# Condition rows loaded first, fourteen of them before the dilated attention, and the attention stores between the two maxima

## What is computed

```python
mod_l = (jax.nn.silu(c) @ w_ada[layer] + b_ada[layer])[:, None, :]
mod_c = jax.nn.silu(c_ctx) @ w_ada[layer] + b_ada[layer]
sh1_l, sc1_l, g1_l, sh2_l, sc2_l, g2_l = jnp.split(mod_l, 6, axis=-1)
...
h_l = modulate(x_l, sh1_l, sc1_l)
```

```python
s_win = jnp.einsum('bhwd,bhrwcd->bhwrc', q_row, k_win).astype(F32) * scale + bias
s_ctx = jnp.einsum('bhwd,bhsd->bhws', q_row, k_ctx).astype(F32) * scale
s = jnp.concatenate([s_win.reshape(b, h, GRID_W, n_win), s_ctx], axis=-1)
p = jax.nn.softmax(s, axis=-1).astype(v.dtype)
...
return (jnp.einsum('bhwrc,bhrwcd->bhwd', p_win, v_win)
        + jnp.einsum('bhws,bhsd->bhwd', p[..., n_win:], v_ctx))
```

## Time and profile before

| | |
|---|---|
| median of 3 runs | 2664.65 us (2660.22 to 2666.28) |
| the profiled execution, its time | 2659.06 us |
| its span, first to last instruction | 2657.3 us |
| busy: PE, DVE, ACT, POOL | 95%, 57%, 35%, 31% of the span |
| mean granted TensorE clock | 0.964 of full speed |
| DVE on condition rows in `dil_project` | 32 instructions, from 49.77 us |
| first scores of the dilated attention | 118.67 us |
| neighbourhood attention | from 1185 to 1291 us |

### The profile page before, as it was taken

The page is one execution under the profiler, slowest core; times in us unless marked ns, Lnnn a source line. Parts: engine busy times, 40 slices in busy tenths (PEclk is TensorE's granted clock), DMA queues, the critical chain, the costliest instruction groups (busy, mean ns, idle before and its releaser), DMA issues.

```text
span 2657.3 us, 37269 instructions
## 1 busy us (share of the span) xinstructions
PE 2515.0 (95%) x14492; PEld 2064.5 (78%) x14492; DVE 1503.9 (57%) x2134; ACT 934.1 (35%) x1414; POOL 834.8 (31%) x445
## 2 busy tenths in 40 slices
PE   6799899999999989998999999999998997999998
PEld 5567887888888877866788888888876755788887
DVE  4756745635755878486455456654675466534242
ACT  3357213322223646335433222122255421433231
POOL 2334002354442222223223333222223321354443
PEclk9899988999997999999999999999998998999999
DMA  5512001434431110231013233422311110232222
GB/s 192 198 41 87 11 1 64 164 134 152 167 134 56 48 48 1 62 74 16 17 48 125 98 111 126 143 88 95 127 64 46 40 72 24 80 111 96 101 96 79
DMA packets 78567, 228.49 MB, mean 86 GB/s; under 512 B 21456, under 2 KB 23504, under 8 KB 77786
## 3 DMA queue, kind: packets, MB, share of 16 engines
q1 hardware_dynamic: 66504, 182.36, 20.0%
q10 hardware_dynamic: 11922, 44.15, 4.9%
HBM read 224.37 MB, written 2.12 MB: 85 GB/s over the span
## 4 chain that ended last, share of the span: by engine, by line
PE 83%; DVE 7%; issue 4%; ACT 3%; POOL 1%; DMA 1%; SPq 0%; DVEq 0%; ACTq 0%; POOLq 0%
PE ps L271 21%; PE ps L272 21%; PE ps L273 21%; PE ps L768 3%; PE ps L783 3%; PE ps L799 2%; PE ps L439 1%; PE ps L391 1%; POOL w_lo L2407 1%; DVE probs L1062 1%; DVE rstd L680 1%; PE ps L2232 1%; DVE small L860 1%; PE ps L448 1%; ACT probs L832 1%
## 5 line engine op out<-in xcount | busy, mean ns | idle before, releaser
L2407 POOL TENSOR_TENSOR w_lo<-ring,w_hi 128x1024 fp32r<-128x1024 f32 x293 | 712.9, 2434 | 1445.6 <-ACT w_hi L264 942.4
L271 PE MATMUL ps<-act_hi,w_hi 128*128 128x512 f32 x2280 | 843.4, 370 | 16.1 <-DVE mix_lo L950 11.0
L273 PE MATMUL ps<-act_hi,w_lo 128*128 128x512 f32 x2280 | 829.9, 364 | 0.0
L272 PE MATMUL ps<-act_lo_ffn,w_hi 128*128 128x512 f32 (+1 forms) x1408 | 512.8, 364 | 0.0
L271 PEld LDWEIGHTS ps<-act_hi,w_hi 128*128 128x128 f32 x2280 | 430.2, 189 | 100.5 <-issue 21.1
L273 PEld LDWEIGHTS ps<-act_hi,w_lo 128*128 128x128 f32 x2280 | 429.0, 188 | 72.2
L264 ACT CAST w_hi<-ring 128x1024 fp32r<-128x1024 f32 (+1 forms) x167 | 174.0, 1042 | 724.9 <-PE ps L273 633.9
L1137 ACT CAST w_hi<-ring 128x1024 fp32r<-128x1024 f32 (+1 forms) x132 | 137.5, 1043 | 459.8 <-PE ps L273 459.8
L272 PEld LDWEIGHTS ps<-act_lo_ffn,w_hi 128*128 128x128 f32 x1408 | 265.1, 188 | 41.9 <-issue 0.7
L271 PE MATMUL ps<-hidden_hi,w_hi 128*128 128x512 f32 x704 | 256.3, 364 | 1.8 <-DVE hidden_lo L1218 1.5
L1062 DVE SCALAR_TENSOR_TENSOR ada_place<-ada_place 128x1024 f32<-128x1024 f32 x160 | 245.6, 1535 | 20.3 <-DMA ada_place<-in_w_ada 6.6
(11 more groups left out here) (369 smaller groups left out, 3387.1 us busy)
## 6 DMA issues: line engine op xcount, KB each, us to landing
ring<-in_w_ffn SPq DMA_DIRECT2D x204, 512.0 KB, 3.2
ada_place<-in_w_ada ACTq DMA_DIRECT2D x80, 512.0 KB, 4.3
ada_place<-in_w_ada SPq DMA_DIRECT2D x16, 512.0 KB, 3.3
ring<-in_w_gdn SPq DMA_DIRECT2D x16, 512.0 KB, 3.2
ring<-in_w_hy SPq DMA_DIRECT2D x12, 512.0 KB, 3.2
ring<-in_w_dil_qk SPq DMA_DIRECT2D x8, 512.0 KB, 6.8
ring<-in_w_out SPq DMA_DIRECT2D x8, 512.0 KB, 3.2
ring<-in_w_diff_qk SPq DMA_DIRECT2D x8, 512.0 KB, 3.2
```

Of the source, the lines that this page charges most:

```text
L271: pe.matmul(out, w[0], x[0], start=start, stop=False)
L272: pe.matmul(out, w[0], x[1], start=False, stop=False)
L273: return pe.matmul(out, w[1], x[0], start=False, stop=stop)
L2407: pool.tensor_tensor(k.w_lo[:, a % SPLITS, :], k.ring[:, a % SLOTS, :], k.w_hi[:, a % SPLITS, :].bitcast(F32), ALU.subtract).then_inc(k.lo ...
```

## The change

The vectors and the first two rows are loaded at the start of the program, behind the fourth weight unit, into `mix_flat`, a buffer that nothing uses that early. All rows of `dil_project` now lie there, products too. `DIL_ROWS` is 14 in place of 16; the shares are two rows behind unit 3 and two behind each of units 6 to 11. VectorE does eleven rows ahead of the bias lines and three behind them. The two rows that are left go to `ffn1`: `Ffn.rows` now gives one row each to the first two output tiles of the third chunk. In the attention stages that are not joined (`dil`, `na`, `gqa`, 56 pairs) the store of pair p - 4 stands ahead of the second maximum.

```diff
@@ PairAttention.vector
+        def store(p):
+            v.eng.wait_ge(self.summed, self.nth(p + 1))
+            v.eng.tensor_copy(self.pairs[p]["out"], k.bank(self.turn_bank(self.use[p]), P)).then_inc(self.stored, 1)
+
...
             if 1 <= p <= N:
                 invert(p - 1, 0)
+            joined = self.pairs[0]["joined"]
+            if p >= 4 and not joined:
+                store(p - 4)
             if p < N:
                 largest(p, 1)
-            if p >= 4:
-                v.eng.wait_ge(self.summed, self.nth(p - 3))
-                v.eng.tensor_copy(self.pairs[p - 4]["out"], k.bank(self.turn_bank(self.use[p - 4]), P)).then_inc(self.stored, 1)
+            if p >= 4 and joined:
+                store(p - 4)
...
-DIL_ROWS = 16
-DIL_LOADS = SLOTS + SPLITS
-DIL_SHARES = {DIL_LOADS + n: (5 * n // 2 + (n > 0), min(5 * (n + 1) // 2 + 1, DIL_ROWS)) for n in range(7)}
+DIL_ROWS = 14
+DIL_SHARES = {SLOTS - 1: (0, 2), **{SLOTS + SPLITS + n: (2 + 2 * n, 4 + 2 * n) for n in range(6)}}
@@ Ffn.rows
         if self.ada == 0:
-            return [DIL_ROWS + (8 if c == 1 else 24) + a] if c == 1 or a < hidden else []
+            row = DIL_ROWS + (8 if c == 1 else 24) + a
+            return [row] if row < ADA else []
...
+def dil_rows(k):
+    return k.view(k.mix_flat, 0, 5, D)
+
+def load_condition(k, eng, place=None):
+    eng.dma_start((k.ada if place is None else place)[:, 0:2, :], bass.AP(k.dram["cond_rows"], 0, [[0, P], [D, 2], [1, D]])).then_inc(k.ada_rows, 16)
@@ dil_project_vector
-    for row in range(DIL_ROWS // 2 + 1):
-        ffn1(k).ada_tile(v, row, product=k.probs.rearrange("p s n -> p (s n)")[:, 0:D])
+    for row in range(11):
+        ffn1(k).ada_tile(v, row, place=dil_rows(k))
...
-    for row in range(DIL_ROWS // 2 + 1, DIL_ROWS):
+    for row in range(11, DIL_ROWS):
@@ dil_project_scalar
-            s.eng.activation(k.ada[:, 0:2, :], k.ada[:, 0:2, :], ACT.Silu).then_inc(k.ada_rows_ready, 1)
+            rows = dil_rows(k)[:, 0:2, :]
+            s.eng.activation(rows, rows, ACT.Silu).then_inc(k.ada_rows_ready, 1)
@@ sync_program
             load(a)
-            if u0 + a == DIL_LOADS:
-                k.after(sp, "norm1")
-                load_condition(k, sp)
-            for row in range(*DIL_SHARES.get(u0 + a, (0,))):
-                f1.ada_load(sp_serial, row)
             if u0 + a == SLOTS - 1:
                 for dst, src in (...):
                     sp.dma_start(dst, src).then_inc(k.loaded_late, 16)
+                load_condition(k, sp, dil_rows(k))
+            for row in range(*DIL_SHARES.get(u0 + a, (0,))):
+                f1.ada_load(sp_serial, row, place=dil_rows(k))
```

More of the change, by code:

```diff
@@ L1027, in per_loop, with ada_load @@
         return 0 if self.ada is None else len(self.rows(c, 0)) + len(self.rows(c, 1))
-    def ada_load(self, s, n, it=0, per=0):
+    def ada_load(self, s, n, it=0, per=0, place=None):
         if self.ada is None:
@@ L1035, in ada_load @@
             s.eng.wait_ge(k.ada_used, it * per + (at - 1))
-        s.eng.dma_start(k.ada[:, 2 + n % 2, :], k.dram[f"w_ada{self.ada}"][it * per + n]).then_inc(k.ada_landed[n % 2], 16)
+        s.eng.dma_start((k.ada if place is None else place)[:, 2 + n % 2, :], k.dram[f"w_ada{self.ada}"][it * per + n]).then_inc(k.ada_landed[n % 2], 16)
     def ada_begin(self, s):
@@ L1052, in ada_rows, with ada_tile @@
         s.eng.activation(k.ada[:, 0:2, :], k.ada[:, 0:2, :], ACT.Silu).then_inc(k.ada_rows_ready, 1)
-    def ada_tile(self, v, n, it=0, per=0, product=None):
+    def ada_tile(self, v, n, it=0, per=0, place=None):
         if self.ada is None:
@@ L1058, in ada_tile @@
         k, at = self.k, ADA * self.ada + n
-        w = k.ada[:, 2 + n % 2, :]
+        place = k.ada if place is None else place
+        w = place[:, 2 + n % 2, :]
         v.eng.wait_ge(k.ada_landed[n % 2], it * (8 * per) + 16 * (at // 2 + 1))
         for q in range(2):
-            ins = v.eng.scalar_tensor_tensor(k.ada[:, 4, :] if product is None else product, w, 1.0, k.ada[:, q, :], ALU.mult, ALU.mult,
+            ins = v.eng.scalar_tensor_tensor(place[:, 4, :], w, 1.0, place[:, q, :], ALU.mult, ALU.mult,
                                              accum_out=k.mod_flat[:, bass.ds(it * (2 * per) + (2 * at + q), 1)])
@@ L1078, in ada_end @@
             link(v, v.eng.tensor_scalar(part, part, 1.0, None, ALU.add))
-def load_condition(k, eng):
-    eng.dma_start(k.ada[:, 0:2, :], bass.AP(k.dram["cond_rows"], 0, [[0, P], [D, 2], [1, D]])).then_inc(k.ada_rows, 16)
+def dil_rows(k):
+    return k.view(k.mix_flat, 0, 5, D)
+def load_condition(k, eng, place=None):
+    eng.dma_start((k.ada if place is None else place)[:, 0:2, :], bass.AP(k.dram["cond_rows"], 0, [[0, P], [D, 2], [1, D]])).then_inc(k.ada_rows, 16)
 def ffn1(k):
```

## The result

| | before | after |
|---|---|---|
| median (lowest to highest) | 2664.04 us (2660.22 to 2666.28) | 2635.57 us (2633.36 to 2639.78), 4 runs |
| ratio of the runs after to those before | | 0.9896, 95% interval 0.9879 to 0.9914 |
| profiled execution: time, span | 2659.06, 2657.3 us | 2635.31, 2633.5 us |
| mean granted TensorE clock | 0.964 | 0.969 |

The change is faster by 28.5 us by the medians (the interval makes that 22.9 to 32.2 us) and by 23.8 us by the two profiled executions. The forecast was 2640 us.

What follows compares the result with a forecast made beforehand. PE bounds most of the span, so gains lie where it idles: the first 120 us and the neighbourhood attention. 2659.06 - 12.5 - 9.3 - 0.5 = 2636.8 us, or 2642.4 from the median; forecast 2640 us, range 2630 to 2652.

Steps and rivals of the forecast that it cites:

- VectorE's start and the wait of ScalarE: Dilated projection: vectors loaded 34 us sooner remove ScalarE's 5.22 us wait before the SiLU; VectorE starts at 44.5 us.
- The early loads at nothing: Program start: 2 MB more in flight ahead of units 4 to 6 end by 32 us, unit 4 wanted at 45: no cost.
- The bias: Dilated projection: two rows fewer and the earlier start let SP issue the bias at 89.4 us, first scores at 103.3 us.
- The 13.9 us behind it: Dilated projection: time from the bias issue to the first scores of the dilated attention, taken as unchanged.
- PE late next: Dilated projection: PE ends at 104.5 us if its clock falls again, else 99.5; first scores at 106.9 us by the first.
- the gap before the bias lines: PE's wait for weight unit 9: shrinks from 4.2 to about 3.2 us; its clock drop costs 5.0 us if it recurs.
- The sum at the start: First scores of the dilated attention 11.8 or 15.4 us sooner; 12.5 us taken.
- The lines hidden by 0.4 us: Eleven rows ahead of the bias lines: lines still come 0.4 us before ScalarE's cast of unit 10; otherwise 1 to 2 us.
- The stores: Neighbourhood attention: eight PE waits each 1.13 us shorter, 9.0 us; clock up to 6.8 us, mask and turned copy against; 9.3 taken.
- Rival (a): Neighbourhood attention: GpSimd's scaling or the turned copy takes over the wait, stores give 2 us, 2647 us in all; chance 0.15.
- The other stages: Dilated attention -0.5 us (between -2 and +2), grouped-query attention 0 (up to 21 us), two rows in ffn1 nothing (up to 5.1).
- The two bases: Same sum taken from the profiled execution, 2636.8 us, and from the median of the runs shown, 2642.4 us; forecast between them.

Runs made afterwards that it cites:

- the start-alone one: The changed kernel with the store put back behind the second maximum, vectors and rows as changed: 2650.19 us, 0.9945 against the kernel before.
- the sixteen rows: The changed kernel with sixteen rows in the dilated projection in place of fourteen, rows 14 and 15 loaded ahead of the bias: 2645.01 us, 0.9928.
- the moved mask: The changed kernel with the neighbourhood window mask on VectorE behind the turned copy in place of ahead of it: 2635.79 us, 0.9904.
- the filled gap: The changed kernel with four 128x512 matmuls, result unused, in PE's idle gap ahead of the bias lines: 2636.12 us, 0.9912.
- the two experiments on the gap: The changed kernel with four unused matmuls in PE's gap (2636.12 us), or with rows 6 and 7 loaded behind weight unit 9 (2636.95 us).
- the kernels with stores alone: The kernel before with only the stores moved: in all three unjoined attention stages (2650.41 us, 0.9944), or in the neighbourhood attention only (2651.63 us, 0.9953).
- the eleven rows: The changed kernel with eleven projection rows, three more in ffn1, unit 9 ahead of rows 6 and 7, nine rows before the lines, bias before unit 11: 2635.77 us.

## Why the prediction was right

**VectorE's start and the wait of ScalarE.** As predicted: no wait in front of the SiLU, first row at 44.76 us (44.5 forecast). With the old place of the load the wait is back.

**The early loads at nothing.** Right in cost, wrong in how: I counted on the DMA engines and not on SP, which the vectors' issue held for 8.34 us. It came out free because the next weight load in SP's list waited for GpSimd anyway: it was issued at 21.28 us, where it was 20.98 us before.

**The bias.** Forecast 89.4 us, measured 90.83 us in the changed kernel, 89.67 in the start-alone one. The 13.9 us behind it were confirmed by the sixteen rows. In the changed kernel this path would give 104.7 us.

**PE late next.** That was the right limit: 106.9 us by the sum with the clock falling again, 107.46 us measured, and ScalarE's last cast waits for PE. The step that was mis-sized is the gap before the bias lines: I let it shrink from 4.2 to 3.2 us, and it was 5.29 us in this trace (3.04 us in the start-alone one). From the issue of unit 9 to its cast it is 6.9 us in this trace and in that of the moved mask, and 4.6 us in those of the start alone and of the filled gap; why it lands at two times is not shown. The clock fell behind the gap either way, to 0.73 over 14.3 us. That is 3.9 us of missing clock where the sum had 5.0, which took back half of what the longer gap cost: PE ended at 105.0 us, 104.5 forecast.

The Trainium skill (TensorE: Matmul & The Clock Gate, section "HAM oscillation — how this bites in real kernels") said that an idle gap which comes back on every pass is paid for on every pass. The traces agree: behind gaps of 3.04 and 5.29 us the granted clock was 0.76 and 0.73 over the next 14.3 us, and 0.88 where the gap was filled. What this clock costs at the first scores is less than the 5.0 us that I gave to it. With the landing of unit 9 alike, the trace with the gap filled has them at 105.16 us and the one without at 105.19 us, since the lines came next.

**The sum at the start.** 12.5 us forecast; 11.2, 11.0 and 13.5 us in three traces that run the same instructions up to there (the changed kernel, the moved mask, the start alone).

**The lines hidden by 0.4 us.** They were kept at 87.08 us and done at 87.89; the cast of unit 10 went ahead at 88.81 us, released by PE: hidden by 0.9 us. In the start-alone kernel, where PE was 2.3 us earlier, and in the two experiments on the gap, the cast of unit 10 waited for the lines, so the small margin was real.

**The stores.** 9.3 us forecast, 10.2 us measured in the changed kernel, 10.3 and 10.2 in the kernels with stores alone. The store's own part was right: "PE's eight waits down to about 4 us" came out at 3.6 us, 9.1 us less, by the 1.13 us each that the sum took. But the number 9.3 is close partly by luck, because two terms that the prediction named and set against each other, without taking a size for either, were both large. Rival (a), the turned copy in the store's place, took back 4.8 us in seven waits, more than half; moving the mask took away all but one of them. And PE's clock came back: 5.9 us less busy time for the same matmuls, nearly the 6.8 us that the prediction gave as the most. Rival (a) priced the stores at 2 us; its wait did come, and without the clock the stores would have given 4.3 us.

**The other stages.** Dilated attention -0.5 us forecast, +0.2 us measured (from the first scores to PE's first matmul of the next stage, 42.3 us before and 42.5 after). Grouped-query attention 0, +0.1 us. `ffn1` 0, 0.0 us by the marks, though its first row landed late.

**The two bases.** The sum was 22.3 us; the traces have 21.4 us in the places named, 2.5 us by the clock in an untouched stretch, and 23.8 us in all. The profiled execution before was 5.0 us below its median and the one after 0.3 us, which makes the 28.5 us of the medians. 2640 us, between the two bases, was too long by 4.4 us. The sum from the profiled execution alone, 2636.8 us, is 1.2 us off, but only with the 2.5 us that no term of it had.

## What to carry to other kernels

A load that waits for its buffer in SP's list holds everything behind it (14.55 us in one kernel here); count what stands behind the row, not only the row. In a double-buffered queue of many small jobs, two jobs fewer ahead of the load that another stage waits for were worth 4.3 to 6.5 us at that stage's start.

A PSUM read that TensorE waits for belongs ahead of work that only later steps need. Where PE has no gap, VectorE can idle for the sum at no cost that the traces show. Price the clock with the waits: here it gave back more (5.9 us) than the waits did (4.3 us).

When a path is shortened, price the next one on the list before adding edits: here the moved mask and the eleven rows won 2.7 and 4.0 us in their own stage, and nothing that the whole could show. And before a gain of 2 us in one trace is put down to an edit, look at a second trace of the same instructions.

## What the runs showed of the hardware

- A DMA of 1 MB that was issued at 7.03 us, behind 5 MB and some smaller transfers issued since 0.75 us, held the issuing engine for 8.34 us; the same issue at 40.90 us in the kernel before took 0.36 us. The traces of the start alone and of the moved mask have 7.76 and 7.78 us for it.
- The same instructions in the same order gave a granted clock of 0.83 in one kernel's trace and 0.86 in another's over the same stage, which took 97.9 and 95.6 us.
- Two waits of PE of 1.65 and 1.53 us, which ended 5.6 us apart, had a granted clock of 0.53 over 3.6 us behind them. With four waits of 0.51, 0.39, 1.07 and 0.28 us in the same steps it was 1.00.
- A gap of 1.70 us at 71 to 73 us had a granted clock of 1.00 from 71 to 77 us in one kernel and 0.74 in another.
- Two traces of one instruction sequence differ by 2.3 us at 105 us from the start, through a gap of 3.04 or 5.29 us behind a 512 KB load.
